# SSD output stage: the next chunk's state sums and the backward offset are issued between exponents and inner products

## The reference, cut to what matters

```
cb     = einsum('bclgn,bcsgn->bclsg', cc, bc)
decay  = exp(where(lower, acum[:, :, :, None] - acum[:, :, None, :], -inf))
y_diag = einsum('bclsg,bclsgr,bcsgrp->bclgrp', cb, decay, xd)
chunk_states = einsum('bclgn,bclgr,bclgrp->bcgrpn', bc, decay_to_end, xd)
h      = h * chunk_decay + chunk_states          # scan over chunks
y_off  = einsum('bclgn,bcgrpn,bclgr->bclgrp', cc, h_starts, exp(acum))
y      = y_diag + y_off                          # once forward, once backward
```

## Time and profile before

| | us |
|---|---|
| three timed runs | 3557.53, 3551.98, 3556.85 (median 3556.85) |
| the profiled execution, its own time | 3558.21 |
| its span, first to last instruction | 3556.5 |
| first to last forward offset but one (14 chunks) | 294.5 |

### The profile page before, as it was taken

One profiled execution on the slowest core, in us unless ns is written; L12 is line 12 of the kernel. 1 busy time (PEld: TensorE's weight loads), 2 busy tenths in 40 slices (PEclk: granted clock), 3 DMA queues, 4 the chain that ended last, 5 costly groups with the idle time before them and its releaser, 6 DMA issues. The chain is left out here.

```text
span 3556.5 us, 37784 instructions
## 1 busy us (share of the span) xinstructions
PE 3269.8 (92%) x15012; PEld 2567.8 (72%) x15012; DVE 1640.7 (46%) x1907; ACT 963.7 (27%) x1795; POOL 348.0 (10%) x226
## 2 busy tenths in 40 slices
PE   7899999998999879994999979999999599999788
PEld 7688888876887647773888858878877355555567
DVE  2754542475024238774444433333342555554355
ACT  2422221111211044441222222233223234433210
POOL 0100000000012035550000000000000001010012
PEclk9999999999999968886999989999999599999899
DMA  4222323432236345543333332223121422210232
GB/s 162 73 70 58 103 95 116 148 112 73 84 126 210 98 134 159 153 139 124 118 107 124 112 128 96 90 89 107 54 89 62 108 53 48 60 36 7 95 119 95
DMA packets 210927, 358.50 MB, mean 101 GB/s; under 512 B 22020, under 2 KB 143492, under 8 KB 202897
## 3 DMA queue, kind: packets, MB, share of 16 engines
q1 hardware_dynamic: 198790, 333.91, 29.2%
q10 hardware_dynamic: 4608, 16.78, 1.3%
q0 software_dynamic: 7392, 5.89, 0.8%
HBM read 234.64 MB, written 121.74 MB: 100 GB/s over the span
## 5 line engine op out<-in xcount | busy, mean ns | idle before, releaser
L634 PE MATMUL p_ps<-hmT_hi,p_w_hi 128*128 128x512 f32 x1312 | 525.4, 400 | 21.5 <-ACT p_work L355 15.9
L634 PE MATMUL p_ps<-hmT_hi,p_w_lo 128*128 128x512 f32 x1312 | 514.7, 392 | 0.0
L634 PE MATMUL p_ps<-hmT_lo,p_w_hi 128*128 128x512 f32 x1312 | 514.0, 392 | 0.0
L1728 PE MATMUL p_ps<-h2T_hi,p_w_hi 128*128 128x512 f32 x800 | 327.2, 409 | 19.2 <-DVE h2T_lo L1590 19.2
L1728 PE MATMUL p_ps<-h2T_lo,p_w_hi 128*128 128x512 f32 x800 | 314.4, 393 | 0.0
L1728 PE MATMUL p_ps<-h2T_hi,p_w_lo 128*128 128x512 f32 x800 | 314.4, 393 | 0.0
L634 PEld LDWEIGHTS p_ps<-hmT_hi,p_w_hi 128*128 128x128 f32 x1312 | 248.7, 190 | 75.7 <-issue 21.1
L634 PEld LDWEIGHTS p_ps<-hmT_hi,p_w_lo 128*128 128x128 f32 x1312 | 248.2, 189 | 53.3
L634 PEld LDWEIGHTS p_ps<-hmT_lo,p_w_hi 128*128 128x128 f32 x1312 | 248.7, 190 | 49.6
L1877 PE MATMUL t_psO<-t_prob,t_v 128*65 128x512 f32 (+3 forms) x640 | 260.8, 530 | 0.9 <-DVE t_out_turned L1979 0.2
L1932 ACT ACTIVATE t_prob<-t_psS 128x1024 f32<-128x1024 f32 (+1 forms) x160 | 150.1, 938 | 320.8 <-PE t_psS L1865 178.0
(11 more groups left out here) (362 smaller groups left out, 5907.0 us busy)
## 6 DMA issues: line engine op xcount, KB each, us to landing
p_w_raw<-in_w_in SPq DMA_DIRECT2D x66, 512.0 KB, 6.1
p_spare<-in_wada ACTq DMA_DIRECT2D x32, 512.0 KB, 5.4
p_spare<-scratch_xs_tok SPq DMA_DIRECT2D x19, 512.0 KB, 4.4
scratch_xs_tok<-p_work SPq DMA_DIRECT2D x8, 1152.0 KB, 6.1
p_work<-in_wada SPq DMA_DIRECT2D x16, 512.0 KB, 3.3
p_work<-in_x SPq DMA_DIRECT2D x16, 512.0 KB, 3.3
scratch_dT<-p_work SPq DMA_DIRECT2D x8, 1024.0 KB, 5.9
scratch_zpT<-p_work SPq DMA_DIRECT2D x8, 1024.0 KB, 4.0
```

What stands on the lines that cost most here:

```text
L634: mm = pe.matmul(PS[:, c, 0:width], wt[n][:, q, :], xx[:, q, cols], start=(q == 0 and j == 0), stop=(q == KT - 1 and j == 2))
L1728: mm = pe.matmul(ps[:, c, :], wt[n][:, q, :], xx[:, q, c * CH:(c + 1) * CH], start=(q == 0 and j == 0), stop=(q == KT - 1 and j == 2))
```

## The change

`sums` and `offset` take a list of groups, so that their four matmuls can be issued one or two at a time. The four matmuls of `sums(c + 1)` move from the end of chunk c into it: one after each of exponent groups 1, 2, 4 and 5. Its waits move with the first of them, its signal with the last. The backward offset is split in two: its first half, with its waits, goes ahead of the last pair of heads, the second half stays behind exponent group 7. Nothing is added or removed, and only PE's list changes.

```diff
--- before.py
+++ after.py
@@ -978,17 +978,19 @@
                               start=True, stop=False)
                     pe.matmul(psE[:, q % 2], ident_r[:], tri_r[:, q // 4].unsqueeze(1).to_broadcast([P, 4, P]), start=False,
                               stop=True).then_inc(S["seg"], 1)
-                def sums(c):
-                    pe.wait_ge(S["weighted"], c + 1)
-                    pe.wait_ge(bt_in[c % 2], 16 * (c // 2 + 1))
-                    if c >= 1:
-                        pe.wait_ge(S["state"], c)
-                    for g in range(GROUPS):
+                def sums(c, groups):
+                    if groups[0] == 0:
+                        pe.wait_ge(S["weighted"], c + 1)
+                        pe.wait_ge(bt_in[c % 2], 16 * (c // 2 + 1))
+                        if c >= 1:
+                            pe.wait_ge(S["state"], c)
+                    for g in groups:
                         mm = pe.matmul(psS[:, g * 256:(g + 1) * 256], bt[c % 2][:, g * NS:(g + 1) * NS],
                                        xw[:, g * 256:(g + 1) * 256], start=True, stop=True)
-                    mm.then_inc(S["summed"], 1)
-                def offset(c, state):
-                    for g in range(GROUPS):
+                    if groups[-1] == GROUPS - 1:
+                        mm.then_inc(S["summed"], 1)
+                def offset(c, state, groups=range(GROUPS)):
+                    for g in groups:
                         mm = pe.matmul(psO[:, g * 256:(g + 1) * 256], cT[c % 4][:, g, :], state[:, g * 256:(g + 1) * 256],
                                        start=True, stop=True)
                     return mm
@@ -1006,7 +1008,7 @@
                     for q in range(8):
                         exponents(c, q)
                     if c == 0:
-                        sums(0)
+                        sums(0, range(GROUPS))
                 pe.wait_ge(S["rows_in"], 112)
                 for c in range(NC):
                     ahead = (lambda q: exponents(c + 2, q)) if c + 2 < NC else (lambda q: None)
@@ -1023,25 +1025,29 @@
                     skipped(0)
                     inside(c, range(0, 4))
                     ahead(0)
+                    beside = (lambda g: sums(c + 1, (g,))) if c + 1 < NC - 1 else (lambda g: None)
                     inside(c, range(4, 6))
                     ahead(1)
+                    beside(0)
                     inside(c, range(6, 8))
                     ahead(2)
+                    beside(1)
                     skipped(1)
                     ahead(3)
                     inside(c, range(8, 10))
                     ahead(4)
+                    beside(2)
                     inside(c, range(10, 12))
                     ahead(5)
+                    beside(3)
                     inside(c, range(12, 14))
                     ahead(6)
+                    pe.wait_ge(S["off_f_read"], c + 1)
+                    pe.wait_ge(h_in[c % 2], 16 * (c // 2 + 1))
+                    offset(c, hb[c % 2], (0, 1))
                     inside(c, range(14, 16)).then_inc(S["inside"], 1)
                     ahead(7)
-                    pe.wait_ge(S["off_f_read"], c + 1)
-                    pe.wait_ge(h_in[c % 2], 16 * (c // 2 + 1))
-                    offset(c, hb[c % 2]).then_inc(S["off_b"], 1)
-                    if c + 1 < NC - 1:
-                        sums(c + 1)
+                    offset(c, hb[c % 2], (2, 3)).then_inc(S["off_b"], 1)
 def walk_tiles(eng, body, tally=None, per=0):
     body(0, 0)
     with eng.Fori(0, LT // 2 - 1) as i:
```

## The result

| | before | with the change |
|---|---|---|
| median of timed runs, us | 3554.41 (4 runs) | 3623.48 (4 runs, 3620.62 to 3639.76) |
| ratio, 95% interval | | 1.0204 [1.0177, 1.0231] |
| profiled execution, us (span) | 3558.21 (3556.5) | 3622.91 (3621.2) |
| 14 chunks, forward offset to forward offset, us | 294.48 | 355.72 |

Ratios leave out executions in a slower state of the chip, so that they can differ from the quotient of the medians; the only one met here is of 3886.08 us, with a mean clock of 0.81, in the run with L958 moved alone. The prediction was 3587, slower, with 3547 to 3620 as range. The direction was right, the size was not: +30 was forecast, +69 was measured. Of the 64.7 between the two profiled executions 61.2 lie in the 14 chunks, so it is there that the loss has to be explained.

What follows compares the result with a forecast made beforehand. PE bounds the loop, its excess being clock. Six chunks at 27.9, seven at 19.3 and one at 21.0 make 323.6 against 294.48, +29; +1 for the last heads gives +30: 3588.2 profiled, 3587 median, range 3547 to 3620.

Steps and rivals of the forecast that it cites:

- What bounds the kernel: In the 14 chunks PE is the bound, busy 294.15 of 294.48 us; time above 17.82 a chunk is clock.
- That the mixture of heads and exponents is at the edge of the clock: Inside a chunk, pairs of heads and exponent groups alone can drop the clock, as after 3.40 us fully busy.
- The chunk's end: At the chunk border, products wait for ACT and the forward offset for DVE's psO read; the waits coincide, 0.5 a chunk.
- The rows for exponent group 0: After the first four heads, PE waits for the last small load: 1.5 us taken, between 0 and 2.4.
- every chunk falls: Rival: the small-load wait is 2.4 and enough alone to drop the clock; +63, 3620 us, chance 0.14.
- The Trainium skill on turns between queues: DMA engines alternate queues packet by packet, so SP's large loads would not delay POOL's small load: wait 0.
- The state: After odd chunks, the first sum needs DVE's state at T + 10.08 (T: backward offset's end): 3.6 us late, 1.6 new.
- no sum would wait for L917: Sign of being wrong: no sum waiting for DVE's state instruction; about six waits of 1.6 to 3.6 us were expected.
- The price of a fall: In each chunk after an odd one, the clock drop costs 6.5 us, between rows of 4.76 and 8.15.
- Chunks after a slow border: Seven chunks starting at low clock get their small loads in time but recover later: 19.3 us each.
- The clock stays up: Rival: matmuls inside the chunk are dense enough despite idle moments; -7 or -19, 3549 or 3538 us, chance 0.15.
- The Trainium skill's rule that idle gaps bring falls: Clock drops come from idle gaps between matmul bursts; by it waits of 0.5 to 1.6 are short.

Runs made afterwards that it cites:

- The order with spread matmuls and no wait but the 0.46 at the border: The change with SP's large loads held until the small loads land and DVE's L958 moved behind the next chunk's decays: 3527.99 us, ratio 0.9917.
- one repair: The change with SP's hb and later loads held until the three small loads have landed: 3601.40 us, ratio 1.0128.
- the other none: The change with DVE's L958 moved behind the next chunk's decays, large loads not held: 3634.28 us, ratio 1.0193.

## Why the prediction was wrong

- *What bounds the kernel*: right. *That the mixture of heads and exponents is at the edge of the clock*: nothing speaks against it. The order with spread matmuls and no wait but the 0.46 at the border holds the clock for 13 chunks, the kernel before does not.
- *The chunk's end*, 0.5: right, 0.46.
- *The rows for exponent group 0*: this is the step that failed. It took a wait of 1.5, with 0 and 2.4 as ends, because `hb` would be issued 0.86 earlier, and it let no fall follow from that wait alone. `hb` was moved from behind the first small load to ahead of it, and the landing got later, not earlier: the prediction did not set the two issue times beside each other (1478.87 of SP and 1478.26 of POOL, 0.61 apart, against a shift of 0.86). Measured: 2.6 to 3.9, nine times, each with a fall. The forecast had six chunks with a fall. In its terms it had 6 x 3.6 + 7 x 0.5 = 25.1 of waiting and 49.0 for the clock; measured are 34.7 and 71.5, the latter with the 4 of a longer chunk. That is the nearest to the rival *every chunk falls*, whose wait was 2.4 and whose time was 3620; it had been given 0.14. Not every chunk fell, nine did, and that its time came within 4 us of the measured one is in part luck.
- *The Trainium skill on turns between queues* (DMA: Bandwidth & Descriptors, section on queues, rings and completion order): as the prediction read that rule, the wait would have been 0. The trace has 6.0 us to landing behind the large loads, against 2.2 with them held.
- *The state*: right in size, T + 10.08, but hidden behind the wait above; it shows only when that is gone. That no sum would wait for L917 was one of the prediction's signs of being wrong, and it came true in the change.
- *The price of a fall*, 6.5 between two rows of before: for the nine chunks of the change it is 7.2 in the mean, so it was the number of falls that was off more than the size. For the falls that it was meant for, those at the state's wait, it was too low: 9.9 in the mean with the loads held. The text had said that the place speaks for the longest row, 8.15, and then took less.
- *Chunks after a slow border*, 19.3: right, 19.2 to 19.4, but there are three of them and not seven.
- *The clock stays up*: right as a mechanism, in a kernel without the waits (3528), wrong for this one. The Trainium skill's rule that idle gaps bring falls (TensorE: Matmul & The Clock Gate, section on HAM oscillation) fits the fall after 1396.30 in kind, and not the one at 1454.50, where PE had no gap.

## What to carry to other kernels

When matmuls are moved from a burst at the border of a loop into its middle, the burst's work as a cover moves too. List every wait that it hid (here an ACT read, a PSUM read, small DMAs, a state on DVE), and set the issue times of DMAs on different queues side by side: a signal that comes 0.9 us earlier let a 512 KB load overtake the first of three small ones that PE needs first, and the small ones landed later. And where two late inputs end at nearly the same point, repair both before judging either; here one repair brought 22 us, the other none, both together 95.

## What the runs showed of the hardware that was not expected

A chunk with the same instructions takes 18.56 us with a wait of 0.46 at its border and 31.43 with one of 2.89 inside it. What is lost is not in a fixed proportion to the wait: against a busy time of 18.10, the nine chunks of the change with a wait of 2.6 to 3.9 lose between 2.1 and 4.8 times its length (24.34 with 2.60 and 0.46 of waiting, 32.52 with 2.98). And the clock falls both ways: after idle time (1399.7) and with PE busy throughout with pairs of heads and exponent groups (1454.50). With all four sums spread among them, no profile shows a fall in a chunk without a wait of over 0.6 us inside it, and in the chunk with the loads held 0.3 us of waiting had passed when the clock fell.
